# Split weights and inner features of a four-layer kernel move to other addresses

## The chip, the cores and the metric

The kernel runs as one program on one core of a Trainium2 chip. The metric is the time of one execution on the device in microseconds; three runs of the kernel before are given, with their median. The profile was taken in one further execution.

## The reference, cut to what matters

Everything is float32, with 256 tokens of width 1024. A first block of two layers runs a hybrid layer (a recurrent unit and retention) and a sparse attention layer, each followed by a gated feed-forward; a second block of two layers adds attention, a Fourier mix and a spatial gate, joined by gates:

```python
def swiglu(x, w1, w3, w2):
    return (jax.nn.silu(x @ w1) * (x @ w3)) @ w2          # hidden width 2816

def first_block(x, ...):
    for layer in range(2):
        hn = rmsnorm(h, attn_norm[layer])
        h = h + (hybrid_ab(hn, ab_w_in, ..., ab_w_out) if layer % 2 == 0
                 else nsa(hn, nsa_w_in, ..., nsa_w_out))
        h = h + swiglu(rmsnorm(h, ffn_norm[layer]), ffn_w1[layer], ffn_w3[layer], ffn_w2[layer])
    return rmsnorm(h, final_norm)

def _merge(h, outs, gates, w_br, w_merge, b_merge, w_out):   # second block, each layer
    yb = jnp.stack([o * jax.nn.silu(z) for o, z in zip(outs, gates)], axis=2)
    y = jnp.einsum('bnrw,rwd->bnrd', yb, w_br)
    g = jax.nn.sigmoid(h @ w_merge + b_merge).reshape(b, n, 4, 1024)
    return jnp.sum(g * y, axis=2) @ w_out
```

Nearly all of the work is in the products of features with weights. In layer 0 of the second block they are made for 512 tokens (256 and 256 of context), elsewhere for 256.

## The kernel before

Features lie transposed in SBUF: 128 features to the partitions, tokens along the free axis. All large weights reach the core as 167 chunks of 128 x 2048 float32 (1 MiB), in the order that the list `FLOW` writes out: `ab_in`, `ab_out`, then `w1_0` and `w3_0` in turns, `w2_0`, `nsa_in`, `nsa_out`, `w1_1` with `w3_1`, `w2_1`, and for each layer of the second block `in`, `merge` (20 chunks) and `out` (4 chunks).

A chunk passes four hands. The SyncE queue loads it in two halves into a ring of four `stage` buffers (`load`). ScalarE rounds each half to fp32r, the high part, in `WH` (`high`, L256). VectorE subtracts that from the raw half and writes the rest, the low part, to `WL` (`low`, L261). TensorE takes blocks of 128 x 128 out of both (`product`). `WH` and `WL` have two buffers each, used in turns, so chunk n+1 is split while chunk n is multiplied. `WH` may be overwritten once the chunk two before is done.

Features are split alike into a high part (`XH`, `HH[:, 0]`) and a low part (`XL`, `HH[:, 1]`). A product is three matmuls into one PSUM bank: high weights by high features (L329), high weights by low features (L330), low weights by high features (L331). Where the result is wanted with tokens on the partitions, features are the stationary operand and weights the moving one (L326 to L328). A feed-forward makes 22 blocks of 128 inner features in `hidden`; w2 multiplies these.

The order on each engine is the order of the code. No planner decides anything.

Addresses follow from the order of the `sb(...)` calls, each with its number of float32 columns per partition. `WH0` comes straight behind `XX` (8448 columns), then `WH1`, `WL0`, `WL1`, `stage`, some small tiles and `arena`. The features have a view that leaves out `HI` = 48 columns ahead of the high part and `LO` = 112 ahead of the low part (`shifted`); `hidden` has the same. Layer 0 of the second block uses `XX0`, which has neither. `hidden`, `merged`, `merged_low` and the low branches lie over parts of `arena`. `early` is a feature tensor of layer 1 with 258 columns to a row.

Functions that the change and the prediction touch:

Of the kernel before, what the change touches and what calls it, by code (L numbers as in the profile page):

```python
# [5 lines left out]
F32 = mybir.dt.float32  # L6
F32R = mybir.dt.float32r
# [6 lines left out]
FNET = 28, 31  # L14
SLOT = 2048
NSTAGE = 4
ARENA = 18608
HI, LO = 48, 112
SWAPPED = ("hq", "hk", "nks", "nkw", "nq0", "nq1", "nq2", "nq3", "k0", "k1")

# [97 lines left out]
def build(nc, A, out):  # L118
    ctx = ExitStack()
    with ctx:  # L120
        def sb(name, cols, dt=F32):
            return ctx.enter_context(nc.sbuf_tensor(name, [128, cols], dt))
# [19 lines left out]
        def shifted(v, n):  # L142
            return v[:, HI:HI + 2 * (n + LO - HI)].rearrange("p (s q) -> p s q", s=2)[:, :, 0:n]
# [2 lines left out]
        XX0 = both[:, 0:8192].rearrange("p (s k n) -> p s k n", s=2, k=8)  # L146
        XX = shifted(both, 4096).rearrange("p s (k n) -> p s k n", k=8)
        XH, XL = XX[:, 0], XX[:, 1]
        WH = [sb(f"WH{i}", 2048, F32R)[:, :] for i in range(2)]
        WL = [sb(f"WL{i}", 2048, F32R)[:, :] for i in range(2)]  # L150
        stage = sb("stage", NSTAGE * 1024)
        MOD = sb("MOD", 100)

# [3 lines left out]
        SM = sb("SM", 640)  # L157

        sb("before_arena", 72)
        with nc.sbuf_tensor("arena_below", [128, 5632], F32), nc.sbuf_tensor("hidden", [128, 11440], F32R) as hid:  # L160
            HH = shifted(hid, 5632).rearrange("p s (a n) -> p s a n", a=22)
        with nc.sbuf_tensor("merged_low", [128, 4096], F32R) as ml, nc.sbuf_tensor("arena_between", [128, 4096], F32):
            with nc.sbuf_tensor("merged", [128, 4096], F32R) as mh, nc.sbuf_tensor("branches_low1", [128, 2048], F32R) as zl1:
                ml, mh, zl1 = ml[:, :], mh[:, :], zl1[:, :]
        arena = sb("arena", ARENA)
        psum = ctx.enter_context(nc.psum_tensor("psum", [128, 4096], F32))
# [23 lines left out]
        def view(at, cols, shape=None, **dims):  # L190
            v = arena[:, at:at + cols]
            return v.rearrange(shape, **dims) if shape else v

        four, two = dict(shape="p (a n) -> p a n", a=4), dict(shape="p (a n) -> p a n", a=2)
# [11 lines left out]
        FLOW = [("ab_in", c) for c in (2, 3, 4, 5, 6, 7, 8, 9, 0, 1, 10, 11)] + [("ab_out", c) for c in range(4)]  # L206
# [5 lines left out]
        for l in range(2):  # L212
            FLOW += [(f"in_{l}", c) for c in ((1, 4, 0, 3, 2, 5), (0, 3, 2, 5, 1, 4))[l] + (8, 9, 10, 6, 7)]
            FLOW += [(f"merge_{l}", c) for c in range(20)]
            FLOW += [(f"out_{l}", c) for c in range(4)]

        def half(m):

            (name, c), lo = FLOW[m // 2], m % 2 * 1024
            j, i = m % NSTAGE, m // 2 % 2  # L220
            return (A[name][c][:, lo:lo + 1024], stage[:, j * 1024:j * 1024 + 1024], WH[i][:, lo:lo + 1024],
                    WL[i][:, lo:lo + 1024], j)

        class Stream:


            def __init__(self):
                self.n = 0
# [7 lines left out]
        def quarter(j):  # L236

            src, raw, hi, lo, _ = half(j // 2)
            return [v[:, j % 2 * 512:j % 2 * 512 + 512] for v in (src, raw, hi, lo)]

        def load(e, m):
            src, raw, _, _, j = half(m)
            if m >= NSTAGE:
                if m < NSTAGE + 2:
                    e.wait_ge(*ve.of(f"hn.low{2 * m - 2 * NSTAGE + 1}"))
                else:
                    e.wait_ge(s_lo, m - NSTAGE - 1)
            e.dma_start(raw, src).then_inc(s_stage[j], 16)

        def high(e, m):  # L250
            _, raw, hi, _, j = half(m)

            e.wait_ge(s_stage[j], 16 * (m // NSTAGE + (j >= 2)))
            if m >= 4 and m % 2 == 0:
                e.wait_ge(*pe.of(f"chunk{m // 2 - 2}"))
            e.activation(hi, raw, ACT.Copy).then_inc(s_hi, 1)  # L256
# [18 lines left out]
        class Chunk:  # L275


            def __init__(self, flow, name, c, blocks=8):
                self.n, flow.n = flow.n, flow.n + 1
                assert FLOW[self.n] == (name, c), (FLOW[self.n], name, c)  # L280
                self.blocks, self.come = blocks, 0
                self.hi, self.lo = [v[self.n % 2].rearrange("p (k c) -> p k c", k=blocks) for v in (WH, WL)]

            def arrive(self, e, k):
                m = 2 * self.n + 1 + (k >= self.blocks // 2)
# [773 lines left out]

        F = Box()  # L1060
        F.hh = [view(4096 + 512 * n, 512, **two) for n in range(3)]
        F.sg = [view(17072 + 512 * n, 512, **two) for n in range(3)]

        def hidden(k):

            return HH[:, :, k, :]

# [2132 lines left out]
```

## Time and profile before

| | us |
|---|---|
| three runs | 1367.22, 1361.17, 1367.77 |
| median | 1367.22 |
| span of the profiled execution, first to last instruction | 1363.3 |
| TensorE busy | 1344.2 |
| VectorE busy | 790.6 |
| ScalarE busy | 640.8 |
| GpSimd busy | 160.1 |

For the profiled execution only the span is given; no time of the whole launch stands beside it. TensorE's matmuls are pipelined: a record reaches from the start of a matmul to its modelled end, and the next one starts before that. So the mean duration of a record is longer than what a matmul adds to the time. That is the distance from one start to the next. The trace shows it in two ways: starts in the timeline, and a stretch of time divided by the number of matmuls in it.

### The profile page before, as it was taken

How to read it: one execution, taken by the hardware profiler on the slowest of the kernel's cores; microseconds unless marked ns; L12 is line 12 of the kernel's file. 1: busy time of each engine (PE TensorE's matmuls, PEld its weight loads, DVE VectorE, ACT ScalarE, POOL GpSimd, SP SyncE). 2: the span in 40 equal slices, each digit the busy share in tenths (PEclk: the TensorE clock that was granted, in tenths of full speed). 3: DMA queues.
4: the chain of work that ended last, by engine and by line, in shares of the span. 5: the costliest groups of instructions: out<-in, count | busy, mean ns of one | idle time of the engine just before them, and what ended most of it. 6: DMA issues, size and time to landing. Idle time of an engine off the chain costs nothing.

```text
span 1363.3 us, 24540 instructions
## 1 busy us (share of the span) xinstructions
PE 1344.2 (99%) x10306; PEld 1200.5 (88%) x10306; DVE 790.6 (58%) x1239; ACT 640.8 (47%) x1126; POOL 160.1 (12%) x131
## 2 busy tenths in 40 slices
PE   9999999999999999999999999999999999999999
PEld 8989999999855899999987777888888888879999
DVE  6976666557767666655724567433333455775554
ACT  6645444444365554455433445323232345555442
POOL 0020111001300012110004000111011100301110
PEclk9999999999999999999999999999999999999999
DMA  8535767556597455665432210222222234414553
GB/s 319 186 124 185 229 226 256 188 186 217 186 336 267 150 190 191 199 197 173 140 115 94 93 56 32 93 93 93 93 93 95 92 122 144 147 61 153 194 186 124
DMA packets 60974, 215.43 MB, mean 158 GB/s; under 512 B 6720, under 2 KB 12736, under 8 KB 57408
## 3 DMA queue, kind: packets, MB, share of 16 engines
q1 hardware_dynamic: 56272, 206.59, 45.4%
q10 hardware_dynamic: 4592, 7.26, 1.5%
q8 instruction: 82, 1.34, 0.4%
q14 instruction: 28, 0.23, 0.1%
HBM read 208.59 MB, written 1.05 MB: 154 GB/s over the span
## 4 chain that ended last, share of the span: by engine, by line
PE 88%; DVE 7%; ACT 3%; issue 1%; DMA 1%; SPq 0%; POOL 0%; ACTq 0%; DVEq 0%; POOLq 0%
PE psum L329 24%; PE psum L330 23%; PE psum L331 23%; DVE WL L261 3%; PE psum L1246 3%; PE psum L1271 2%; PE psum L1409 2%; PE psum L326 1%; PE psum L327 1%; PE psum L328 1%; ACT WH L256 1%; PE psum L2714 1%; PE psum L1602 1%; DMA stage<-ab_in 1%; PE psum L1250 1%
## 5 line engine op out<-in xcount | busy, mean ns | idle before, releaser
L329 PE MATMUL psum<-XX,WH 128*128 128x256 f32 (+1 forms) x1912 | 584.7, 306 | 8.2 <-DVE WL L261 2.8
L331 PE MATMUL psum<-XX,WL 128*128 128x256 f32 (+1 forms) x1912 | 576.3, 301 | 0.0
L330 PE MATMUL psum<-XX,WH 128*128 128x256 f32 (+1 forms) x1912 | 576.3, 301 | 0.0
L261 DVE TENSOR_TENSOR WL<-stage,WH 128x1024 fp32r<-128x1024 f32 x332 | 397.1, 1236 | 254.9 <-ACT WH L256 254.7
L256 ACT ACTIVATE WH<-stage 128x1024 fp32r<-128x1024 f32 x332 | 333.4, 1052 | 330.1 <-PE psum L331 286.0
L329 PEld LDWEIGHTS psum<-XX,WH 128*128 128x128 f32 x1912 | 359.4, 188 | 39.7 <-issue 13.8
L331 PEld LDWEIGHTS psum<-XX,WL 128*128 128x128 f32 x1912 | 359.9, 188 | 15.9
L330 PEld LDWEIGHTS psum<-XX,WH 128*128 128x128 f32 x1912 | 358.8, 188 | 15.7 <-issue 0.5
L329 PE MATMUL psum<-hidden,WH 128*128 128x256 f32 x352 | 97.5, 277 | 0.0
L331 PE MATMUL psum<-hidden,WL 128*128 128x256 f32 x352 | 97.2, 276 | 0.0
L330 PE MATMUL psum<-hidden,WH 128*128 128x256 f32 x352 | 97.2, 276 | 0.0
L2883 POOL TENSOR_TENSOR arena<-arena,con 128x512 f32<-128x512 f32 (+1 forms) x48 | 43.0, 895 | 385.6 <-DVE con L2801 385.0
L1371 ACT ACTIVATE arena<-psum,SM 128x16 f32<-128x16 f32 (+3 forms) x144 | 67.6, 482 | 2.3 <-DVE SM L1303 2.3
L329 PEld LDWEIGHTS psum<-hidden,WH 128*128 128x128 f32 x352 | 66.1, 188 | 0.4 <-issue 0.4
L330 PEld LDWEIGHTS psum<-hidden,WH 128*128 128x128 f32 x352 | 66.1, 188 | 0.0
L331 PEld LDWEIGHTS psum<-hidden,WL 128*128 128x128 f32 x352 | 66.1, 188 | 0.0
L1197 POOL TENSOR_TENSOR arena<-arena,SM 128x512 f32<-128x512 f32 x22 | 42.6, 1936 | 182.1 <-ACT arena L1164 182.1
L1356 ACT ACTIVATE arena<-psum 128x512 f32<-128x512 f32 (+2 forms) x48 | 32.9, 685 | 61.8 <-PE psum L1271 57.0
L2801 DVE TENSOR_TENSOR con<-psum,con 128x512 f32<-128x512 f32 (+1 forms) x48 | 26.3, 555 | 57.8 <-ACT con L2641 29.8
L2641 ACT ACTIVATE con<-psum,par 128x512 f32<-128x512 f32 (+1 forms) x64 | 35.6, 574 | 43.9 <-PE psum L331 43.9
L1300 DVE TENSOR_REDUCE SM<-psum 128x2 f32<-128x1024 f32 (+4 forms) x48 | 41.8, 872 | 20.2 <-PE psum L1246 12.2
L326 PE MATMUL psum<-WH,XX 128*128 128x256 f32 x176 | 49.9, 283 | 0.4 <-DVE WL L261 0.4
(288 smaller groups left out, 1675.7 us busy)
## 6 DMA issues: line engine op xcount, KB each, us to landing
stage<-w SPq DMA_DIRECT2D x132, 512.0 KB, 4.6
stage<-merge SPq DMA_DIRECT2D x80, 512.0 KB, 4.5
ring<-ada SPq DMA_DIRECT2D x24, 1024.0 KB, 7.0
stage<-in SPq DMA_DIRECT2D x44, 512.0 KB, 4.5
stage<-ab_in SPq DMA_DIRECT2D x22, 512.0 KB, 5.8
stage<-nsa_in SPq DMA_DIRECT2D x20, 512.0 KB, 4.8
stage<-out SPq DMA_DIRECT2D x16, 512.0 KB, 4.2
stage<-ab_out SPq DMA_DIRECT2D x8, 512.0 KB, 4.7
```

The costliest lines, as they stand in the source:

```text
L256: e.activation(hi, raw, ACT.Copy).then_inc(s_hi, 1)
L261: e.tensor_tensor(lo, raw, hi.bitcast(F32), ALU.subtract).then_inc(s_lo, 1)
L326: e.matmul(dst, xh, wh, start=start, stop=False)
L329: e.matmul(dst, wh, xh, start=start, stop=False)
L330: e.matmul(dst, wh, xl, start=False, stop=False)
L331: return e.matmul(dst, wl, xh, start=False, stop=stop)
L1197: e.tensor_tensor(F.sg[c % 3], F.sg[c % 3], spread(RT, 2, 256), ALU.mult).then_inc(*gp.tick(f"{p}.gate{c}"))
L1246: t = e.matmul(v[:, q, h, :], query(h)[r], key[r], start=h == 0 or u.mask is None, stop=u.mask is None)
L1300: e.tensor_reduce(nm, scored(p, n, u), AX.X, ALU.max, negate=True).then_inc(*ve.tick())
L1371: e.activation(s[:, q, h, :], v[:, q, h, :], ACT.Exp, bias=nm[:, q, h:h + 1], scale=rate, accum_out=sm[:, q, h:h + 1]).then_inc(*ac.tick(f ...
L2641: e.activation(L.SG[n % 2], banks[f"g{l}.{m}.{i}"][:, 0:L.NT], ACT.Sigmoid, bias=P("b_merge", l * 32 + MERGED[i] * 8 + m)).then_inc(*ac.ti ...
L2883: e.tensor_tensor(L.M[:, m, :], L.M[:, m, :], L.T2[n % 2], ALU.add).then_inc(*gp.tick(f"u{l}.{n}"))
```

## The change

The two `WH` and the two `WL` buffers become 128 columns longer each, and a chunk n is put `offset(n)` columns into its buffer, high and low part alike. The offset depends on the stage and on the chunk's number c in it: 8c (w1_0 and w2_0), 8c + 4 (w3_0, w2_1), 8c + 40 (w1_1), 8c + 44 (w3_1), c (merge_1), 32c (out_1), and 0 in all others. A column is 4 bytes. `hidden` starts 8 columns (32 bytes) further on within its place. The tile `F.sg` of the feed-forward moves from the end of `arena` to column 2048, and `arena` ends earlier. `WH1` moves by 512 bytes, `WL0` by 1024, `WL1` by 1536, and all behind them, `arena` included, by 2048.

No engine gets another instruction, another wait or another order: listed row for row, the programs differ only in the source lines, which are 18 higher from `Chunk` on.

```diff
@@ -14,7 +14,8 @@
 FNET = 28, 31
 SLOT = 2048
 NSTAGE = 4
-ARENA = 18608
+ARENA = 17080
+SLACK = 128
 HI, LO = 48, 112
 SWAPPED = ("hq", "hk", "nks", "nkw", "nq0", "nq1", "nq2", "nq3", "k0", "k1")
 
@@ -146,8 +147,8 @@
         XX0 = both[:, 0:8192].rearrange("p (s k n) -> p s k n", s=2, k=8)
         XX = shifted(both, 4096).rearrange("p s (k n) -> p s k n", k=8)
         XH, XL = XX[:, 0], XX[:, 1]
-        WH = [sb(f"WH{i}", 2048, F32R)[:, :] for i in range(2)]
-        WL = [sb(f"WL{i}", 2048, F32R)[:, :] for i in range(2)]
+        WHS = [sb(f"WH{i}", 2048 + SLACK, F32R)[:, :] for i in range(2)]
+        WLS = [sb(f"WL{i}", 2048 + SLACK, F32R)[:, :] for i in range(2)]
         stage = sb("stage", NSTAGE * 1024)
         MOD = sb("MOD", 100)
 
@@ -157,8 +158,8 @@
         SM = sb("SM", 640)
 
         sb("before_arena", 72)
-        with nc.sbuf_tensor("arena_below", [128, 5632], F32), nc.sbuf_tensor("hidden", [128, 11440], F32R) as hid:
-            HH = shifted(hid, 5632).rearrange("p s (a n) -> p s a n", a=22)
+        with nc.sbuf_tensor("arena_below", [128, 5632], F32), nc.sbuf_tensor("hidden", [128, 11448], F32R) as hid:
+            HH = shifted(hid[:, 8:11448], 5632).rearrange("p s (a n) -> p s a n", a=22)
         with nc.sbuf_tensor("merged_low", [128, 4096], F32R) as ml, nc.sbuf_tensor("arena_between", [128, 4096], F32):
             with nc.sbuf_tensor("merged", [128, 4096], F32R) as mh, nc.sbuf_tensor("branches_low1", [128, 2048], F32R) as zl1:
                 ml, mh, zl1 = ml[:, :], mh[:, :], zl1[:, :]
@@ -214,12 +215,29 @@
             FLOW += [(f"merge_{l}", c) for c in range(20)]
             FLOW += [(f"out_{l}", c) for c in range(4)]
 
+        def offset(n):
+
+            name, c = FLOW[n]
+            up = ("w1", "w3").index(name[:2]) if name[:2] in ("w1", "w3") else None
+            if name[-1] == "0":
+                return (8 * c + 4 * up) % 128 if up is not None else 8 * c if name[:2] == "w2" else 0
+            if name[:2] in ("w1", "w3"):
+                return (8 * c + 4 * up + 40) % 128
+            if name[:2] == "w2":
+                return 8 * c + 4
+            return c if name == "merge_1" else 32 * c if name == "out_1" else 0
+
+        def weights(n):
+
+            a = offset(n)
+            return WHS[n % 2][:, a:a + 2048], WLS[n % 2][:, a:a + 2048]
+
         def half(m):
 
             (name, c), lo = FLOW[m // 2], m % 2 * 1024
-            j, i = m % NSTAGE, m // 2 % 2
-            return (A[name][c][:, lo:lo + 1024], stage[:, j * 1024:j * 1024 + 1024], WH[i][:, lo:lo + 1024],
-                    WL[i][:, lo:lo + 1024], j)
+            j, (hi, low) = m % NSTAGE, weights(m // 2)
+            return (A[name][c][:, lo:lo + 1024], stage[:, j * 1024:j * 1024 + 1024], hi[:, lo:lo + 1024],
+                    low[:, lo:lo + 1024], j)
 
         class Stream:
 
@@ -279,7 +297,7 @@
                 self.n, flow.n = flow.n, flow.n + 1
                 assert FLOW[self.n] == (name, c), (FLOW[self.n], name, c)
                 self.blocks, self.come = blocks, 0
-                self.hi, self.lo = [v[self.n % 2].rearrange("p (k c) -> p k c", k=blocks) for v in (WH, WL)]
+                self.hi, self.lo = [v.rearrange("p (k c) -> p k c", k=blocks) for v in weights(self.n)]
 
             def arrive(self, e, k):
                 m = 2 * self.n + 1 + (k >= self.blocks // 2)
@@ -1059,7 +1077,7 @@
 
         F = Box()
         F.hh = [view(4096 + 512 * n, 512, **two) for n in range(3)]
-        F.sg = [view(17072 + 512 * n, 512, **two) for n in range(3)]
+        F.sg = [view(2048 + 512 * n, 512, **two) for n in range(3)]
 
         def hidden(k):
 
```

## Rows read from the trace of the kernel before

**Rows 1.** The page: busy time of each engine, and TensorE's granted clock in 40 slices.
```profile
PE 1344.2 (99%) x10306; PEld 1200.5 (88%) x10306; DVE 790.6 (58%) x1239; ACT 640.8 (47%) x1126; POOL 160.1 (12%) x131
...
PEclk9999999999999999999999999999999999999999
```

**Rows 2.** The page: the chain that ended last, by engine and by line.
```profile
PE 88%; DVE 7%; ACT 3%; issue 1%; DMA 1%; SPq 0%; POOL 0%; ACTq 0%; DVEq 0%; POOLq 0%
PE psum L329 24%; PE psum L330 23%; PE psum L331 23%; DVE WL L261 3%; PE psum L1246 3%; PE psum L1271 2%; PE psum L1409 2%; PE psum L326 1%; PE psum L327 1%; PE psum L328 1%; ACT WH L256 1%; PE psum L2714 1%; PE psum L1602 1%; DMA stage<-ab_in 1%; PE psum L1250 1%
```

**Rows 3.** Table of stretches: us, then busy time and instruction count by engine.
```profile
core 0: us, PE busy (x) PEld busy (x) DVE busy (x) ACT busy (x) POOL busy (x), PEclk, DMA share, GB/s
133.00:301.00 168.00, 168.00 (x1485) 168.00 (x1484) 100.89 (x119) 79.71 (x108) 20.45 (x11) 1.00 0.66 219
495.00:611.00 116.00, 116.00 (x1026) 116.00 (x1025) 72.28 (x87) 54.29 (x75) 20.01 (x10) 1.00 0.60 194
685.00:690.00 5.00, 5.00 (x44) 5.00 (x44) 2.58 (x3) 3.33 (x5) 0.00 (x0) 1.00 0.05 16
900.00:1084.00 184.00, 184.00 (x814) 152.35 (x813) 63.20 (x73) 56.70 (x75) 24.63 (x22) 1.00 0.30 98
1232.00:1360.00 128.00, 128.00 (x1089) 128.00 (x1088) 69.45 (x90) 58.85 (x84) 18.81 (x28) 1.00 0.53 172
```

**Rows 4.** Groups by line, 133 to 301 us: count | busy, mean ns.
```profile
line engine op names shapes xcount | busy us, mean ns | idle before us <-releasers
L330 PE MATMUL psum<-XX,WH 128*128 128x256 f32 x319 | 88.0, 276 | 0.0
L330 PE MATMUL psum<-hidden,WH 128*128 128x256 f32 x176 | 48.6, 276 | 0.0
```

**Rows 5.** Groups by line, 1232 to 1360 us.
```profile
L330 PE MATMUL psum<-XX,WH 128*128 128x256 f32 x240 | 67.4, 281 | 0.0
L261 DVE TENSOR_TENSOR WL<-stage,WH 128x1024 fp32r<-128x1024 f32 x44 | 52.0, 1222 | 36.5 <-ACT WH L256 36.5
L256 ACT ACTIVATE WH<-stage 128x1024 fp32r<-128x1024 f32 x44 | 44.1, 1051 | 41.5 <-PE psum L331 41.5
L330 PE MATMUL psum<-merged_low,WH 128*128 128x256 f32 x63 | 17.7, 281 | 0.0
```

**Rows 6.** Groups by line, 467 to 471.5 us (nsa_out chunk 2).
```profile
L330 PE MATMUL psum<-XX,WH 128*128 128x256 f32 x14 | 3.9, 281 | 0.0
```

**Rows 7.** Groups by line, 473 to 478 us (nsa_out chunk 3).
```profile
L330 PE MATMUL psum<-XX,WH 128*128 128x256 f32 x15 | 4.1, 276 | 0.0
```

**Rows 8.** Groups by line, 685 to 690 us (in_0, values).
```profile
L327 PE MATMUL psum<-WL,XX 128*128 128x256 f32 x15 | 4.2, 283 | 0.0
```

**Rows 9.** Timeline of TensorE, ten rows: start us, us, instruction.
```profile
start us, us, engine line op out<-in xcount [idle before <-releaser]
685.43 0.28 PE L326 MATMUL psum<-WH,XX 128*128 128x256 f32 x1
...
686.51 0.28 PE L326 MATMUL psum<-WH,XX 128*128 128x256 f32 x1
```

**Rows 10.** Groups by line, 1136.5 to 1146.8 us (in_1, 512 columns).
```profile
L330 PE MATMUL psum<-XX,WH 128*128 128x512 f32 x15 | 5.9, 395 | 0.0
```

**Rows 11.** Groups by line, 900 to 1084 us (merge_0, out_0).
```profile
L330 PE MATMUL psum<-XX,WH 128*128 128x512 f32 x192 | 74.7, 389 | 0.0
```

**Rows 12.** The chain in order of time: start us, us, what.
```profile
774.85 0.87 PE psum L1271 x8
```

**Rows 13.** Timeline of TensorE in in_1's `early` products, sixteen rows.
```profile
1117.79 0.29 PE L331 MATMUL psum<-early,WL 128*128 128x258 f32 x1
...
1119.59 0.28 PE L331 MATMUL psum<-early,WL 128*128 128x258 f32 x1
```

## The prediction, made before the changed kernel had run

> **What bounds the kernel now.** I read the page's busy times first: TensorE is busy for 1344.2 of 1363.3 us and is granted its full 2.4 GHz throughout [rows 1]. The chain of waits confirms it: 88% of the span is TensorE, 70% the three product lines L329 to L331, and the weight split on VectorE is 3% [rows 2]. The change leaves every engine's instructions and their order as they are and moves only where operands lie, so the question is what one product matmul costs, stage by stage.
>
> Second, the table of stretches. A matmul's record (276 ns and more) is longer than its turn, so its mean duration is no cost; the turn is the time from one start to the next, which is stretch over count less about 3 records that hang over the edges. In layer 0's feed-forward: 168.00 us / 1482 = 113.4 ns. In layer 1's: 116.00 / 1023 = 113.4. In merge_1 and out_1: 128.00 / 1086 = 117.9 [rows 3]. All three have 256 moving columns, 106.7 ns at 2.4 GHz. So the first two lose 6.7 ns a matmul, the third 11.2. The mean durations carry a fingerprint of this: 276 ns beside a turn of 113.4 [rows 4], 281 beside 117.9 [rows 5], 283 in in_0, where ten rows of the timeline span nine turns, 1.08 us / 9 = 120.0 ns each [rows 8, 9].
>
> Third, what picks the turn. Two neighbouring chunks of nsa_out, same code and the same addresses modulo 8 KiB, run at 281 and at 276 [rows 6, 7]; TensorE stood still between them. So at this placement two steady turns exist, a short one of 113.4 and a long one of 117.9; a restart throws the dice, and the stream keeps what it got: 1482 matmuls the one, 1086 the other. The placement counts too. With "distance" I mean the start of the weights less the start of the moving operand, modulo 512 bytes (steps of k and column halves are 512 or 1024 bytes, so it holds for a stage). WH0 begins 33 KiB behind XX. In ffn and in layer 1 the high features start 48 columns into XX or hidden: distance -192 for WH over XH; WL over XL is 448 bytes short (112 columns). In layer 0 of the second block nothing is shifted: both distances 0. There all 256-column products stand at 120.0 [rows 8, 9], with no second turn; and the 512-column ones are at 184.00 us / 811 = 226.9 ns with record 389 [rows 3, 11], against 395 for 512 columns at -192 [rows 10]. A better distance for one width is a worse one for the other, so distance is a real knob and its effect is not monotonic.
>
> **The change, part by part.** (1) merge_1 and out_1: distance -192 + 4c for c up to 19, so at most -116; out_1 -192, -64, 64, 192. These are the 1152 matmuls of the last 140 us, now at the long turn. If the changed distance ends the long turn, the stretch from 1232 to the end, 131.3 us, shrinks by 131.3 x (1 - 113.4/117.9) = 5.0 us. If it makes it the 120.0 turn, it grows by 131.3 x (120.0/117.9 - 1) = 2.3. The nearest rows, equal placement with either turn [rows 6, 7], are compatible with both ends; I take -5.0, since the distance now moves at every chunk, 24 times, and the long turn would have to survive each move.
>
> (2) The feed-forward layers: 3168 matmuls at 113.4, the short turn [rows 3, 4]. w1_0/w3_0 go from -192 to +144 in steps of 16 bytes, w1_1/w3_1 from -32 to +304, w2 from -224 or -208 upward by 32 a chunk (hidden's own 32 bytes are in this). Low operands stay 256 bytes behind. From below: they keep 113.4 (0 us). From above: all at 120.0, 3168 x 6.6 ns = 20.9 us. I take 0: the short turn held for 1482 matmuls through the change from XX to hidden, while ScalarE and VectorE wrote the other buffer, and nothing dislodged it.
>
> (3) Odd chunks: WH1 moves 512 bytes, WL0 1024, WL1 1536: same distance modulo 512. Both column halves (512 apart) of a chunk have shown both turns, so 0; bounds as in (2). Stages with offset 0 (ab, nsa, in, merge_0, out_0) otherwise keep their distances: 0, with the dice as before.
>
> (4) ScalarE and VectorE write WH and WL at addresses that are no longer on 16 bytes in merge_1. In that stretch the split takes 1051 and 1222 ns a half chunk; ScalarE is busy for 58.85 and VectorE for 69.45 of 128 us [rows 3, 5]. What hides a slower write is that slack: ScalarE's 44 copies could double (+46 us) before it filled the stretch; VectorE's 44 likewise (+54). Between ends of 0 and +100% of a copy's time the span moves by 0.
>
> (5) F.sg moves below F.hh. Its producers and readers wait as before, and GpSimd's 22 products on it have slack: 0.
>
> Sum: 1363.3 - 5.0 = 1358.3 us of span. The profile gives no time of the whole launch beside the span; the three timed runs are 1361.17 to 1367.77 with median 1367.22, 3.9 above the span. What lies around the span is at least 0 and, if the fastest run was one in which the last stretch was fast as well, at most 1361.17 - 1358.3 = 2.9. I take 1.5, and round to **1360 us**. That the median is not 1364.8 fits the dice: layer 0's feed-forward alone at the long turn costs 168.00 x (117.9/113.4 - 1) = 6.7 us, and the runs lie 6.1 and 6.6 apart. So the forecast rests on the short turn in all three long stretches.
>
> The Trainium skill, SBUF — State Buffer, "Who interferes with whom", speaks against the change: TensorE reads moving data and weights through two independent ports and never waits on anyone. By that rule no placement could matter and the sum would be 0. The 120.0 in every unshifted 256-column product, against 113.4 and 117.9 elsewhere, says that it does not hold here as it stands.
>
> **Rivals.** *B: placement does not choose the turn, restarts do.* For: rows 6 and 7 have equal distances and differ. Against: no 276 anywhere at distance 0. Then the time is again a draw: 1363.3 + 1.5 = 1364.8 with today's draw, 1358 to 1371 in all, a median near 1366.
>
> *C (slower): the moving distances walk the feed-forward through the bad one.* Distance 0 has the turn of 120.0 [rows 8, 9], and `early`, whose high distances run from 0 to -56 in steps of 8, is at 1.80 us / 15 = 120.0 too, for 258 columns, where 107.5 + 6.7 = 114.2 would be the good turn [rows 13]. The new table passes 0 in every feed-forward stage. Against: in those rows the low distance is near 0 also, or 64 off, here it is 256 off. If half of the 3168 matmuls go there: +10.5 us, less up to 5.0: 1370 to 1375. It outweighs the gain in the last stretch from 5.0 / 0.0066 = 760 matmuls on, a quarter of them.
>
> *D: the 6.7 ns are themselves a collision.* Eight records of L1271, 128 columns of plain fp32 in what must be two passes (106.7 ns), take 0.87 us: 108.8 each [rows 12]. If the walk takes the products to that, 4320 x 4.6 ns = 19.9 us and the 5.0 go: 1340. Against: no product of 256 or 512 columns in the trace ever ran below 113. The skill's TensorE: Matmul & The Clock Gate, "Wait — 56ns, not 53.3ns?", has N / 2.4 GHz + 2.5 ns as the warm turn, 109.2 for 256; its result would be about the same, and in L1271 the trace comes near it.
>
> **How the numbers follow.** A (forecast) 0.38, B 0.27, C 0.22, D 0.13. A 0.5% change is 6.8 us, about what a measurement of this kernel can tell from none: below 1360.4 is faster, above 1374.1 slower. A lies at that edge (0.23 faster, 0.15 same, since every small stage still throws its dice, 1358 to 1363); B gives 0.03, 0.21, 0.03; C 0, 0.03, 0.19; D 0.13. Together 0.39 faster, 0.39 same, 0.22 slower. For eight in ten the range runs from 1351, which leaves out most of D, to 1373, the middle of C.
>
> **What would show it.** Right: L329 to L331 over XX and merged at 276 in the last 130 us, and 276 in both feed-forwards. B: 281 in one of the three long stretches, for its whole length across many changes of chunk. C: means between 277 and 283 in the feed-forward that change from chunk to chunk with c, worst where the distance is near 0. D: records under 276 and turns under 113. The forecast is wrong if the last stretch stays at 281, or if a stretch that stands at 276 now does not keep it; a copy of L256 much over 1051 ns with TensorE waiting for L261 in merge_1 would sink item (4).

## The result

| | median us | runs | lowest to highest |
|---|---|---|---|
| before | 1367.49 | 4 | 1361.17 to 1368.52 |
| changed | 1381.06 | 4 | 1380.6 to 1381.73 |

The ratio is 1.0115 with a 95% interval of 1.0089 to 1.0141: the change costs 13.6 us, about 1%. The forecast was 1360; the time is rival C's, and above C's own price.

The profiled execution took 1380.8 us with a span of 1378.9, so 1.9 lie around the span. Its table of stretches (us, then busy time and count by engine) answers to [rows 3]. The stretches are w1_0/w3_0 from within w3_0's chunk 0 on, w2_0, w1_1/w3_1 from within w3_1's chunk 0 on, and merge_1 from chunk 1 on with out_1:

```profile
130.00:247.70 117.70, 117.70 (x997) 117.70 (x997) 70.35 (x83) 53.60 (x76) 21.35 (x12) 1.00 0.66 221
247.70:310.00 62.30, 62.30 (x529) 62.30 (x528) 33.34 (x39) 28.34 (x38) 0.00 (x0) 1.00 0.56 186
496.00:613.70 117.70, 117.70 (x999) 117.70 (x998) 70.53 (x84) 54.42 (x74) 21.27 (x11) 1.00 0.56 184
1245.70:1375.90 130.20, 130.20 (x1106) 130.18 (x1104) 70.36 (x91) 60.34 (x85) 18.80 (x28) 1.00 0.52 169
```

Less 3 records at the edges, the turns (the time from one matmul's start to the next) are 118.4, 118.4, 118.2 and 118.0 ns. Before they were 113.4 in the feed-forwards and 117.9 at the end. TensorE is never idle in these stretches and its clock is fully granted (the 1.00), as before. So the loss is neither a wait nor the clock: the same matmuls take longer turns. Stage by stage, from the start of a stage to the start of the next, the first feed-forward went from 182.1 to 189.6 us and the second from 184.0 to 191.4, together +14.9; merge_1 and out_1 grew by 0.1 (141.4 to 141.5). Of the span's +15.7, taken before rounding, that leaves about +0.7 for the short stages.

Groups by line in the first feed-forward and in the last stretch (count | busy, mean ns), which answer to [rows 4, 5]:

```profile
L348 PE MATMUL psum<-hidden,WH 128*128 128x256 f32 x176 | 49.4, 281 | 0.0
...
L279 DVE TENSOR_TENSOR WL<-stage,WH 128x1024 fp32r<-128x1024 f32 x44 | 52.0, 1222 | 37.0 <-ACT WH L274 37.0
L274 ACT ACTIVATE WH<-stage 128x1024 fp32r<-128x1024 f32 x44 | 44.2, 1053 | 41.9 <-PE psum L349 41.9
```

276 has become 281 over `hidden`. The record's mean is a rough sign only: 281 stood beside 117.9 in the kernel before and stands beside 118.4 here. The split in merge_1 takes what it took (1222 and 1053 ns, before 1222 and 1051) although it now writes at steps of 4 bytes.

A mean over a stretch hides what happens in it. Here are the first and the last matmul of two chunks in the timeline of TensorE (start us, us), w3_0's chunk 2 and w1_0's chunk 4, 48 matmuls each:

```profile
151.22 0.28 PE L347 MATMUL psum<-XX,WH 128*128 128x256 f32 x1
156.86 0.28 PE L349 MATMUL psum<-XX,WL 128*128 128x256 f32 x1
...
168.41 0.28 PE L347 MATMUL psum<-XX,WH 128*128 128x256 f32 x1
173.74 0.28 PE L349 MATMUL psum<-XX,WL 128*128 128x256 f32 x1
```

5.64 us / 47 = 120.0 ns in the one, 5.33 / 47 = 113.4 in the other. Their distances are -112 and -64. The turn changes from chunk to chunk, and the values come back with the distance: w1_1 at distance +64 has 113.4 again, at +192 too.

### The profile page after: what moved, and what is told of

It reads as the page before. It is cut to its first block, busy times and chain, and to the rows that moved or that the text cites. A ratio compares the mean times of both kernels' runs of the same rounds, so it can differ in the third digit from the quotient of the medians.

```text
span 1378.9 us, 24540 instructions
## 1 busy us (share of the span) xinstructions
PE 1357.4 (98%) x10306; PEld 1213.5 (88%) x10306; DVE 791.7 (57%) x1239; ACT 641.2 (47%) x1126; POOL 160.0 (12%) x131
## 4 chain that ended last, share of the span: by engine, by line
PE 88%; DVE 7%; ACT 3%; issue 1%; DMA 1%; SPq 0%; POOL 0%; ACTq 0%; DVEq 0%; POOLq 0%
PE psum L347 24%; PE psum L349 24%; PE psum L348 24%; DVE WL L279 3%; PE psum L1264 3%; PE psum L1289 2%; PE psum L1427 2%; PE psum L344 1%; PE psum L346 1%; PE psum L345 1%; ACT WH L274 1%; PE psum L2732 1%; PE psum L1620 1%; DMA stage<-ab_in 1%; PE psum L1268 1%
## 5 line engine op out<-in xcount | busy, mean ns | idle before, releaser
L347 PE MATMUL psum<-hidden,WH 128*128 128x256 f32 x352 | 99.1, 282 | 0.0
L348 PE MATMUL psum<-hidden,WH 128*128 128x256 f32 x352 | 98.8, 281 | 0.0
L1374 ACT ACTIVATE arena<-psum 128x512 f32<-128x512 f32 (+2 forms) x48 | 32.9, 685 | 62.5 <-PE psum L1289 57.0
```

The costliest lines, as they stand in the source:

```text
L347: e.matmul(dst, wh, xh, start=start, stop=False)
L348: e.matmul(dst, wh, xl, start=False, stop=False)
```

## The distance decides, modulo 256 bytes

Put in order by distance modulo 256, the undisturbed chunks of 256 columns give one curve. It is worked out from starts in the traces of the changed kernel and of the experiments below; a chunk's first nine matmuls are left out. That 256 bytes is the period shows in pairs of the changed kernel that lie 256 apart: -112 and +144 both have 120.0, -64 and +192 both 113.3. It is not 128: 0 and 128 differ, 120.0 against 118.7. From here on a distance is given modulo 256.

| distance | 0 | 16 | 32 | 48 | 64 | 80 | 96 | 112 |
|---|---|---|---|---|---|---|---|---|
| turn, ns | 120.0 | 118.4 | 118.3 | 117.8 | 113.3 or 117.8 | 118.7 | 117.3 to 120.0 | 119.9 to 120.2 |

| distance | 128 | 144 | 160 | 176 | 192 | 208 | 224 | 240 |
|---|---|---|---|---|---|---|---|---|
| turn, ns | 118.7 | 118.3 to 120.0 | 120.0 | 118.1 | 113.3 or 117.8 | 116.7 | 116.6 to 117.8 | 117.3 to 120.0 |

The kernel before has -192 = 64 in all of these stages. Of 16 multiples of 16 bytes only 64 and 192 know the short turn. The changed table visits all of them, and only the few feed-forward chunks that land on 64 or 192 had a chance of it. The distance is not everything: at 64, 96, 144, 192, 224 and 240 the same distance showed more than one turn. At 64 it largely follows the chunk before (see entries); what decides at the others was not looked into.

## The experiments

Two theories stood against each other first. Distance: the turn follows from weight start less feature start. Stepping: any change of distance from chunk to chunk unsettles the stream. A third, that the displaced buffers do it, had to be shut out.

### slack_only

```diff
         def offset(n):
...
+            return 0
...
-            HH = shifted(hid[:, 8:11448], 5632).rearrange("p s (a n) -> p s a n", a=22)
+            HH = shifted(hid[:, 0:11440], 5632).rearrange("p s (a n) -> p s a n", a=22)
```

> Keeps the longer buffers, the shorter arena and the new place of F.sg; all offsets are 0 and hidden starts where it did. Distance theory (the turn of a matmul follows from weight start less feature start, modulo 256 bytes): the feed-forwards stand at 113.4 or 117.9 again as before, time 1361 to 1369. Rival, that the displaced buffers (WH1 by 512 bytes, arena by 2048) cause the loss: feed-forward turns over 118, 1375 to 1381.

Measured: 1365.05 us (12 runs, 1360.6 to 1368.86), before 1366.14 (23 runs), ratio 0.9989 [0.9973, 1.0004]. All three long stretches of its profile are at 113.4, span 1359.0 (167.00 us / 1473, 116.00 / 1023, 110.00 / 969):

```profile
134.00:301.00 167.00, 167.00 (x1476) 167.00 (x1475) 100.87 (x119) 79.21 (x108) 19.93 (x10) 1.00 0.65 218
495.00:611.00 116.00, 116.00 (x1026) 116.00 (x1025) 72.82 (x87) 54.13 (x75) 19.94 (x10) 1.00 0.58 193
1243.00:1353.00 110.00, 110.00 (x972) 109.98 (x971) 61.63 (x78) 52.63 (x75) 17.00 (x26) 1.00 0.55 182
```

No cost of the displaced buffers and of the new place of `F.sg` can be seen.

### ffn_only

```diff
-            return c if name == "merge_1" else 32 * c if name == "out_1" else 0
+            return 0
```

> The changed kernel without its offsets in merge_1 and out_1. Distance theory: both feed-forwards as in the changed kernel, 182.1 -> 189.6 us and 184.0 -> 191.3, so +14 to +15 us on the short-turn draw: 1377 to 1382; the last stretch at 113.4 or 117.9 as drawn. Rival, that the last stretch holds part of the loss: under 1375.

Measured: 1380.57 us (4 runs, 1375.83 to 1383.56), ratio 1.0092 [1.0074, 1.0110]. The feed-forwards repeat the changed kernel chunk for chunk (w3_0 at 118.9 on average without its first chunk, w2_0 at 118.1, w2_1 at 118.6 where no wait disturbed it). The whole loss is there, 14.4 us over before, with the offsets at the end gone.

### tail_only

```diff
         def offset(n):
             name, c = FLOW[n]
...
+            return c if name == "merge_1" else 32 * c if name == "out_1" else 0
...
+            HH = shifted(hid[:, 0:11440], 5632).rearrange("p s (a n) -> p s a n", a=22)
```

> Only merge_1 and out_1 keep their offsets. Distance theory: feed-forwards at one of the two old turns; merge_1 near 118.2 and out_1 near 115.6 on average as in the changed kernel, so 0 to +5 us against before where before drew 113.4 in the last stretch, 0 where it drew 117.9: 1363 to 1370. Rival, that stepping the distance frees the stream: merge_1 at 113.4, 1358 to 1364.

Measured: 1368.51 us (12 runs, 1365.13 to 1373.17), before 1366.14, ratio 1.0014 [0.9999, 1.0029]. The table of stretches of its profile, from chunk 3 of merge_1 on:

```profile
1242.00:1358.00 116.00, 116.00 (x982) 116.00 (x982) 63.27 (x81) 54.66 (x78) 18.83 (x28) 1.00 0.54 178
```

116.00 / 979 = 118.5 ns. The rival is out: stepping does not free the stream, it takes the chance of 113.4 away at most offsets.

### hold_or_step

```diff
         def offset(n):
             name, c = FLOW[n]
...
+            if name in ("w1_0", "w3_0", "w2_0"):
+                return 4
+            if name in ("w1_1", "w3_1", "w2_1"):
+                return 32 * (n % 4)
+            return 0
```

> Layer 0's feed-forward holds one offset of 16 bytes in all chunks (distance -176, never changing). Layer 1's steps by 128 bytes at every chunk, through -192, -64, 64, 192, all of them 64 modulo 128. Distance theory: layer 0 at 118.7 throughout; layer 1 at 113.4 or 117.7, never above. Stepping theory (a change of distance at each chunk is what unsettles the stream): the reverse, layer 0 at 113.4 or 117.9 and layer 1 above 118.

Measured: 1373.09 us (one run; before on the same chip 1366.14). Table of stretches, layer 0 (held at 80, which the expectation calls -176) and layer 1 (stepping by 128):

```profile
134.00:309.00 175.00, 175.00 (x1476) 175.00 (x1475) 101.00 (x119) 79.66 (x108) 20.21 (x11) 1.00 0.63 208
515.00:600.00 85.00, 85.00 (x752) 85.00 (x751) 54.09 (x64) 41.19 (x56) 14.90 (x8) 1.00 0.58 192
```

175.00 / 1473 = 118.8 ns without any step, 85.00 / 749 = 113.5 with a step at every chunk (modulo 256 it goes to and fro between 64 and 192). This run decides between the two theories: a bad distance that never changes has a long turn, and changes between good ones do no harm. The groups by line bear it out, 282 against 276:

```profile
L345 PE MATMUL psum<-XX,WH 128*128 128x256 f32 x319 | 90.0, 282 | 0.0
...
L345 PE MATMUL psum<-XX,WH 128*128 128x256 f32 x251 | 69.3, 276 | 0.0
```

Layer 1 did not begin at the short turn. Chunk 1 of w1_1 and of w3_1 stood at 117.8, and the turn changed where w1_1's chunk 2 begins, at the step from 192 to 64:

```profile
512.32 0.28 PE L345 MATMUL psum<-XX,WH 128*128 128x256 f32 x1
514.56 0.28 PE L346 MATMUL psum<-XX,WL 128*128 128x256 f32 x1
514.67 0.28 PE L344 MATMUL psum<-XX,WH 128*128 128x256 f32 x1
516.15 0.28 PE L345 MATMUL psum<-XX,WH 128*128 128x256 f32 x1
```

2.24 us / 19 = 117.9 before it, 1.48 / 13 = 113.8 behind it, with no standstill between. In out_1 of the changed kernel and of tail_only the same step from 192 to 64 did the same. So a step can change the turn that a good distance has.

### hidden_only

```diff
         def offset(n):
...
+            return 0
```

> All offsets 0; only hidden starts 32 bytes later, so that the distance in both w2 stages is -224 and everywhere else as before. Distance theory: w2_0 and w2_1 at 118.3 (the value of the changed kernel's w2_0 chunk 0, also at -224), w1/w3 at 113.4 or 117.9; w2_0 takes 62.5 us instead of 59.8. Rival, that the start of an operand on a 64-byte line counts and not the distance: hidden now starts on one, so w2 at 113.4 or less.

Measured: 1372.72 us (one run, before 1365.39). Table of stretches, w2_0:

```profile
243.00:305.00 62.00, 62.00 (x526) 62.00 (x525) 33.34 (x39) 28.32 (x38) 0.00 (x0) 1.00 0.57 187
```

62.00 / 523 = 118.5 ns; from start to start of the stages w2_0 took 62.5 us and w2_1 64.2. The 32 bytes alone, without any offset, cost 2.6 and 2.5 us. The weights and those who write them did not move here, the features did, and the turn is the 118.3 that w1_0 of the changed kernel had at distance 32 with its weights moved and its features not. So it is the difference that counts. The rival, that a start on a 64-byte line helps, is out.

### map_pairs

```diff
         def offset(n):
...
+            p = n - 16 if n < 64 else n - 64 + 33
+            if name[:2] in ("w1", "w2", "w3"):
+                return 8 * (p // 8 % 8), 8 * (p % 8)
+            if name == "merge_1":
+                return 0, 4 * c
+            return 0, 0
...
-            a = offset(n)
-            return WHS[n % 2][:, a:a + 2048], WLS[n % 2][:, a:a + 2048]
+            a, b = offset(n)
+            return WHS[n % 2][:, a:a + 2048], WLS[n % 2][:, b:b + 2048]
```

> High and low weights get offsets of their own: in the feed-forwards chunk p = 0..63 has the high weights at 32 x (p // 8) bytes and the low ones at 32 x (p mod 8), from the distance -192; merge_1 keeps the high ones and moves the low ones by 16 bytes a chunk. If every pair (features being read, weights being loaded) has to keep 64 modulo 128: 113.4 or 117.7 only where both offsets are multiples of 128, four chunks of each 64, and 117 to 120 elsewhere. Rival, that only the high pair counts, which two matmuls of three have: whole rows of 113.4 wherever the high offset is a multiple of 128. Turns under 113 anywhere would say that the remaining 6.7 ns are a collision as well.

Measured: 1379.05 us (one run, before 1365.39). The first and last of 38 matmuls in chunk 20 (high pair at 64, low pair at 192), and of 35 in chunk 22 (64 and 0), in the timeline:

```profile
145.26 0.28 PE L345 MATMUL psum<-XX,WH 128*128 128x256 f32 x1
149.46 0.28 PE L346 MATMUL psum<-XX,WH 128*128 128x256 f32 x1
...
156.83 0.29 PE L346 MATMUL psum<-XX,WH 128*128 128x256 f32 x1
160.99 0.28 PE L347 MATMUL psum<-XX,WL 128*128 128x256 f32 x1
```

4.20 / 37 = 113.5 and 4.16 / 34 = 122.4, the worst found. With the high pair at 64, merge_1 had 113.3 only where the low pair was at 64 or 192, and 116.7 to 119.0 at the other offsets. So the place of the low weights counts as well. Nowhere was a turn under 113.3. (192, 64) and (192, 192) came out at 118.9 and 117.8, one chunk each.

### one_detour

The theory leaves open why a stretch at a good distance takes 113.3 in one execution and 117.8 in another. In the changed kernel the turn at 64 was short behind both chunks at 48; behind other distances it was sometimes short and sometimes long. Four detours make use of this:

```diff
         def offset(n):
...
+            return 60 if n in (18, 66, 92, 145) else 0
```

> All chunks at the old distances but four, one behind the last standstill of each long stretch (w1_0 chunk 1, w1_1 chunk 1, w2_1 chunk 6, merge_1 chunk 2), which lie 16 bytes short of them (48 modulo 256 instead of 64). In the changed kernel a stream that came from 48 into 64 took the short turn each of the four times it did so. If that holds, all three long stretches run at 113.4 in every execution: 1358.3 + 1.9 us, plus 4 x 48 x 4 ns = 0.8: 1360 to 1363, with a narrow spread, and faster than before's median of 1366 by 4 to 6 us. Rival, that only a standstill sets the turn and a change of distance is not felt once the old one is back: a spread as before, 1361 to 1370.

Measured: **1362.47 us** (12 runs, 1360.77 to 1365.07), before 1367.11 (17 runs, 1361.39 to 1371.42), ratio 0.9975 [0.9964, 0.9986]. Groups by line before the detour, in it and behind it (merge_1 chunk 1; chunk 2; from chunk 3 on):

```profile
L339 PE MATMUL psum<-XX,WH 128*128 128x256 f32 x10 | 2.8, 281 | 0.0
...
L340 PE MATMUL psum<-XX,WH 128*128 128x256 f32 x14 | 3.9, 280 | 0.0
...
L339 PE MATMUL psum<-XX,WH 128*128 128x256 f32 x216 | 59.6, 276 | 0.0
```

Here the draw had fallen on the long turn, and the detour turned it: from 281 to 276 at the same distance. It beats both kernels: before by 0.25%, measured side by side, and the changed one (1381.06, timed in another job) by about 1.3%; and the spread is 4.3 us instead of 10.0. With `F.sg` and the arena moved it carries more of the change than it needs; slack_only says that these are free. The two were never timed side by side, and their intervals against before overlap, so a gain over slack_only itself is not shown.

### map_512

```diff
         def offset(n):
...
+            if name == "in_0":
+                return 16 if n in (97, 98, 104) else 8 * (n % 4)
+            if name == "merge_0":
+                return 4 * c
+            if name == "out_0":
+                return 80 + 8 * c
+            return 60 if n in (18, 66, 92, 145) else 0
```

> With the same four chunks, and in layer 0 of the second block, where features have 512 columns and the distance is 0: keys and values (256 columns) get 64 bytes, merge_0 walks from 0 to 304 by 16 bytes a chunk, out_0 from 320 by 32. If the rule for 256 columns (64 modulo 128 is the best) holds as it is: keys and values at 113.4 or 117.7 instead of 120.0, merge_0 best at 64 and 192. In_1's 233 ns at distance 64 against 227 at 0 speak for the rival, that 512 columns have their best at 0 modulo 128 and nothing under 226.7 is found.

Measured: 1368.38 us (one run, before 1367.11). The first and last of 28 matmuls of merge_0 at distance 0, of 27 at 64, and of 38 of in_0's products with 256 columns at 64:

```profile
1029.65 0.39 PE L346 MATMUL psum<-XX,WH 128*128 128x512 f32 x1
1035.77 0.39 PE L346 MATMUL psum<-XX,WH 128*128 128x512 f32 x1
...
892.84 0.39 PE L347 MATMUL psum<-XX,WH 128*128 128x512 f32 x1
898.90 0.39 PE L346 MATMUL psum<-XX,WH 128*128 128x512 f32 x1
...
751.79 0.28 PE L343 MATMUL psum<-WH,XX 128*128 128x256 f32 x1
755.98 0.28 PE L344 MATMUL psum<-WL,XX 128*128 128x256 f32 x1
```

226.7, 233.1 and 113.2 ns. For 512 columns the best distances are 240 and 0 (226.7 behind a chunk's first matmuls), then 192 (228.9); the rest has 230 to 234. 16 had 226.7 behind a chunk at 0, but 233.3 in merge_0's chunk 1, near a wait. The rival held in the main: the rule for one width is not that for the other, and nothing is under 226.7. Its "0 modulo 128" did not: 128 has 233. 256 columns in in_0 get from 120.0 to 113.2 or 118.

### detour_and_keys

```diff
         def offset(n):
...
+            if n in (97, 98, 104):
+                return 16
+            return 60 if n in (18, 66, 92, 145) else 48 if n == 136 else 0
```

> one_detour, and three chunks of in_0 with 256 columns (keys, values) 64 bytes further, where the map had 114.4 instead of 120.0, and the one chunk of in_1 with 512 columns at distance 0 instead of 64 (226.7 instead of 233). Distance theory: 288 x 5.5 ns + 48 x 6.5 ns = 1.9 us less than one_detour: 1360 to 1361, before at 1366 to 1367. Rival, that TensorE's waiting for operands in in_0 and in_1 swallows it: as one_detour, 1362.5.

Measured: 1362.95 us (12 runs, 1360.79 to 1364.3), before in the same job 1363.83 (17 runs, 1360.97 to 1375.94), ratio 0.9985 [0.9965, 1.0004]. No gain over one_detour can be shown. In its profile in_0 takes 156.9 us instead of 157.8: chunk 9 stood at the long turn (117.8) throughout and the two others in their second half, so about half of the expected 1.6 us came. The chunk of in_1 took 229.3 ns a matmul, not the expected 226.7. And out_1, which no detour guards, drew the long turn:

```profile
L341 PE MATMUL psum<-merged,WH 128*128 128x256 f32 x35 | 9.8, 281 | 0.0
```

This run also says how far one_detour can be relied on. The same four detours are in it, and no gain over before is clear of the noise, for before's own median was 1363.8 here against 1367.1. The narrow spread came again: 3.5 us against before's 15.0.

### entries

```diff
         def offset(n):
...
+            if (name[:2] in ("w1", "w2", "w3") or name == "merge_1") and n % 2 == 0:
+                return 4 * (n // 2 * 5 % 32)
+            return 0
```

> In the feed-forwards and merge_1 every odd chunk is at the good distance 64, every even one at another multiple of 16 (all of them modulo 256, each about three times), so that each odd chunk shows the turn taken on coming from that distance. If coming from 48 is what gives the short turn, 113.4 stands behind 48 and 117.7 behind some others (behind 0 or 96, say). Rival, that any chunk off the good distance does it: 113.4 in all odd chunks.

Measured: 1372.15 us (one run, before 1363.83). The same good distance behind 16 and behind 96, in the groups by line:

```profile
L344 PE MATMUL psum<-XX,WL 128*128 128x256 f32 x15 | 4.2, 281 | 0.0
...
L344 PE MATMUL psum<-XX,WL 128*128 128x256 f32 x15 | 4.1, 276 | 0.0
```

Short in every case behind 32, 48, 96, 112, 128, 144, 192, 208, 224 and 240 (two or three chunks each; for 48 it is 18 of 18 with the changed kernel, ffn_only and the 12 detours in three traces); long in every case behind 0, 16, 80 and 176 (two or three each). Behind 160 it was long twice and short once. In the changed kernel and ffn_only, one of two chunks behind 32 was long. So neither "any detour" nor "only 48": the distance left decides, though not quite alone. My example of 96 was wrong, 0 was right.

## Why the prediction was wrong, point by point

- **What bounds the kernel**: right. The turn of the product matmuls set the time, on the chain and without waits.
- **The two turns at the old distance, and the draw at a standstill**: right. slack_only's profile drew 113.4 in all three long stretches, before's profile in two.
- **Distance modulo 512**: wrong, and it misled. The period is 256 (the pairs above). The "low operands stay 256 bytes behind", which I held against rival C, is then no difference at all: every feed-forward chunk had the low pair at the same distance as the high one, just as in_0 with its 120.0.
- **Item (2), feed-forwards at 0 us**: this step failed. I reasoned that nothing had dislodged the short turn so far; but nothing had changed the distance so far, XX and hidden having the same one. With bounds of 0 and +20.9 from rows, the value was taken at the end that had no row for it: the only other distances that the trace held for this width, 0 and those of `early`, all had 120. Measured +14.9, by turns of 118.2 to 118.4 in place of 113.4: of the multiples of 16 that the feed-forwards now visit only 64 and 192 have the short turn, and a stretch that is simply held at another one has a long turn too (hold_or_step, 118.8).
- **Item (1), -5.0 us at the end**: wrong too, +0.1. The thought was that a step might break the long turn. A step can, from 192 to 64 for one, but in merge_1 each step led to a distance with a turn of its own, 116.7 to 122.2 at all but two of them (76 and 88, 113.3).
- **Item (3)**: right (slack_only). **Item (4)**: right, the writes kept their times. **Item (5)**: right.
- **1.5 us around the span**: 1.9 measured, within the bounds.
- **Rival C**: the mechanism, with too narrow a reach. I let half of the matmuls meet distance 0 and priced +10.5. The table meets 0 in four chunks only, 192 of 3168 matmuls, and in w2_1 not at all, though the prediction has it in every stage. Distance 0 is one bad place among many, and all but two of sixteen cost 3.3 to 6.9 ns a matmul.
- **Rival B** falls as stated: placement does choose the turn, and of the multiples of 16 only 64 and 192 leave a draw between 113.3 and 117.8. **Rival D** falls: 113.3 is the least in every map. Its yardstick was weak: L1271 is a transpose, and that its 108.8 ns are two passes no run shows. The Trainium skill (TensorE: Matmul & The Clock Gate, "Wait — 56ns, not 53.3ns?") gives a warm turn of N / 2.4 GHz + 2.5 ns. The estimate from it for 256 columns, 109.2, was not reached by any fp32r product of 256 columns here.
- The Trainium skill (SBUF — State Buffer, "Who interferes with whom") has TensorE waiting on nobody, with independent ports for moving data and weights. The measurement decides: the same products took 113.3 to 122.4 ns by where their operands lay. That a matmul's reading meets the load of the next weights is a guess. XH and XL lie a multiple of 256 bytes apart, and so do the two halves of `hidden`, so the runs cannot tell the weights being loaded from those being multiplied. The mechanism stays open.

## What to carry to other kernels

Where TensorE is busy all the time and still slower than its columns, take the turn from start to start, not the record's duration, and look at it chunk by chunk. Weights and features of a product have a good distance, one for each width; keep it in every stage and through both buffers, and find it by walking offsets over the chunks of one run, which costs one run for 60 values. If a trace holds a single good value of a parameter, every new value is to be priced by the rows off it.

## What the hardware showed that I had not expected

- The turn of a 128x128 by 256-column fp32r matmul depends on the distance between operand starts modulo 256 bytes: 113.3 to 122.4 ns, with differences down to steps of 4 bytes (merge_1: 120.0 at 84, 113.3 at 88, 118.2 at 92). In nearly all chunks the turns repeat within a nanosecond from trace to trace; at 76 they did not, 113.3 in the changed kernel and 120.0 in tail_only.
- For 512 columns the good distance is another: 226.7 ns at 0, 233 at 64.
- At 64 and 192 there are two steady turns, 113.3 and 117.8 ns. A standstill draws one, and a chunk of 48 matmuls at another distance can set it: behind 16 bytes less, the short one followed 18 times of 18. Four such chunks in 167 gave 1362.5 us against 1367.1 in one_detour; in detour_and_keys only the narrower spread was clear.
